# Seven-product pairs moved to other places in the second feed-forward matrix and in the first step for v

## The chip, the cores and the metric

One core of one Trainium2 chip runs the whole program. The metric is the device time of one execution in microseconds (us). The kernel before takes 2172.05 us, the median of 3 runs (2170.63 to 2173.68).

## The reference

For 256 tokens of width 2048 in float32, a transformer block with two mixers is followed by a gated mixer block. Of the many matrix products only three stretches matter here:

- feed-forward input: `silu(h Wg) * (h Wu)`, with h (256 x 2048) and two matrices of 2048 x 5632;
- feed-forward output: `x = x + ff W2`, with ff (256 x 5632) and W2 (5632 x 2048);
- second block: `h = rmsnorm(x)`, then `h [u | v | gate]`, a matrix of 2048 x 12288 of which the v part (2048 x 4096) is computed first, and an output product.

Between the last two lies an RMS norm over the rows of x: h is x transposed, times a gain by channel, and the factor by token is applied to the products' results.

## The kernel before, in words

**Weights.** Every matrix streams through a ring of four slots (`raw`, RING = 4). A *unit* is 256 rows by 512 columns (512 KB). For unit n, SyncE's queue issues the load of `raw` (L460) once `lo_ready` says that the unit four before it in the same slot has been split (L456). ScalarE (ACT) makes the rounded part `w_hi` (L580), VectorE (DVE) the remainder `w_lo` (L1109), and TensorE (PE) multiplies: each float32 product is three matmuls (hi x hi, hi x lo, lo x hi; `three`, L2059). ACT and DVE work four units ahead: at place j of a step they split unit j + 4. ACT does it only when PE has used unit j (`unit_used`), since that frees the slot's `w_hi`.

**Pairs.** In the feed-forward and in the second block, units come in pairs u (units 2u and 2u + 1: the same 256 rows, two blocks of 512 columns). A *plain pair* (`plain_pair`, L2072) is 8 products of 128 x 128 by 128 x 512, 24 matmuls. A *mixed pair* (`mixed_pair`, L2110) gets the same result from seven products of sums of blocks, 21 matmuls. For that DVE makes four sums of weight blocks (`weight_sums`, L1511: `t_sum`, L1528 to L1531; one of them is written back into `raw`), ACT rounds them (`t_hi`, L919), and DVE takes the remainder (`t_lo`, L1541). On the activation side there are sums too. Where the operand is h they are made once, when a block of rows is turned: `stat_hi` (L854, L858) on ACT, `stat_lo` (L1447, L1451 to L1454) on DVE, `mixed_hi` (L864) on ACT, `mixed_lo` (`s_lo`, L1461) on DVE, whose `op_ready` tells PE that the block is there. Where the operand is ff they are made for each mixed pair: `sf_sum` (L1523 to L1526), `sf_hi` (L922), `sf_lo` (L1544); PE waits for `sf_ready` ahead of the pair's second unit (L2130). `weight_sums` for pair u runs at place j = 2u - 4, and needs both units of the pair in `raw`; `t_lo` and `sf_lo` follow at place 2u - 3. Plain pairs of the feed-forward output also need `ff_hi` (L579) and `ff_lo` (L1108), one of each for two units.

**Which pairs are mixed** is written out by hand. The feed-forward output (segment FFN_OUT) has 2 steps of 22 pairs (44 units), with the mixed pairs in `MIXED_OUT`. The product for v (V_IN) has 4 steps of 8 pairs (16 units): `MIXED` = (2, 4, 6), but (4, 6) in step 0. Three PSUM regions gather the mixed products; after a step's last mixed pair, ACT and DVE copy and add them (`parts`, L926 and L1546), and DVE adds them to x (`rows_with_parts`, L1574). At the end of the step `rows_whole` (L1586) adds the rest from the accumulators `gp` and gives them free for the next step.

**Turning x.** The four blocks of 512 columns of x are ready two by two: blocks 0 and 1 when step 0 of FFN_OUT ends, blocks 2 and 3 when step 1 ends. So blocks 0 and 1 are turned in step 1 of FFN_OUT, and 2 and 3 in step 0 of V_IN. PE transposes a block at a place written by hand (`turn_x`, L2012, at the end of unit j = 1 and of unit j = 4, `turn_rows`, L2159; 8 transposes, L1994). It waits for `op_ready` of the blocks before, since the block's sums share buffers, and ACT and DVE take it up at hand-written places behind their own splits: `rows_hi` (L965) and `rows_lo` (L1637). The first mixed pair of a step waits in `shared_banks` (L2089) for all the turned blocks, because the transposes go through the same PSUM banks as the mixed products. In V_IN every pair u also waits for its own rows of h (L2143).

**The token factor** for v needs the squares of all four blocks of x: `squares(3)` on ACT, `mean_square` and `token_scale` on DVE, a square root on ACT between them, all at hand-written places in `v_first` (L993, L1658). Its user is the evacuation of V_IN's first step.

Of the kernel before, what the change touches and what calls it, by code (L numbers as in the profile page):

```python
# [48 lines left out]
MIXED = (2, 4, 6)  # L49
MIXED_FIRST = (4, 6)  # L50
MIXED_LAST = (2, 4)
MIXED_OUT = ((3, 7, 11, 15, 19), (6, 10, 14, 18))
PLACES = 3


# [38 lines left out]
def build(nc, x, w_in, b_gate, norm_mix, norm_ffn, lb_logits, out_gain, q_gain, k_gain, rel_bias,  # L94
# [3 lines left out]
    with ctx:  # L98
# [254 lines left out]
        QF, IV, G_IN, QK, GATES, PROJ_A, PROJ_B, OUT, FFN_IN, FFN_OUT, V_IN, UG_IN, Y_OUT = range(len(S))  # L353
# [7 lines left out]
        op0, hi0, n, n_hi = {}, {}, 0, 0  # L361
# [5 lines left out]
        TURN_M, TURN_H2, TURN_FF, TURN_H3, TURN_Y = 0, 4, 8, 8 + S[FFN_IN].steps, 12 + S[FFN_IN].steps  # L367
# [14 lines left out]
        def mixed(k, i):  # L382

            if k == FFN_OUT:
                return MIXED_OUT[i]
            if isinstance(i, int) and i == 0 and k != UG_IN:
                return MIXED_FIRST
            if isinstance(i, int) and i == S[k].steps - 1 and k == UG_IN:
                return MIXED_LAST
            return MIXED  # L390

        done_steps, done_pairs = {}, {}
        for k in (FFN_IN, FFN_OUT, V_IN, UG_IN):
            done_steps[k] = sum(S[q].steps for q in done_steps)
            done_pairs[k] = sum(len(mixed(q, i)) for q in done_pairs for i in range(S[q].steps))
# [5 lines left out]
        def pairs(k, i, n):  # L401

            if isinstance(i, int) and i == 0:
                return n + done_pairs[k]
            return i * len(MIXED) + (n + len(mixed(k, 0)) - len(MIXED) + done_pairs[k])

        def last_unit(k, i):

            return 2 * mixed(k, i)[-1] + 1
# [17 lines left out]
        def sums_made(i, n):  # L427

            return (0, len(MIXED_OUT[0]))[i] + n + 1

# [135 lines left out]
        def _(act):  # L566
# [71 lines left out]
            def rms(dst, src, dim):  # L638

                return act.activation(dst, src, ACT.Sqrt, scale=1.0 / dim, bias=eps_c[0:dst.shape[0]])  # L640
# [192 lines left out]
            def scaled_rows(k, i, b):  # L833

                act.wait_ge(bank_free[b], freed(k, i + 1))
                n = 2 * i + b
                for t in range(TB):
                    ins = act.activation(xs_tok[:, t], x_tok[:, t, n * NB:(n + 1) * NB], ACT.Copy, scale=rx[:, t:t + 1])
                ins.then_inc(xs_ready, 1)

            def squares(n):

                for t in range(TB):
                    ins = act.activation(wide4[:, t * NB:(t + 1) * NB], x_tok[:, t, n * NB:(n + 1) * NB], ACT.Square,
                                         accum_out=ssf[:, t, n:n + 1])
                own.link(ins)
                if n == 3:
                    act.sem_inc(sq_ready, 1)

            def stat_hi(n, turn, gain):  # L850

                act.wait_ge(tile_turned, turn + n + 1)
                for m in range(4):
                    ins = act.activation(a_hi[:, 4 * n + m], turn_b[:, m], ACT.Copy, scale=col(gain + 4 * n + m))  # L854
                if n:
                    act.wait_ge(op_ready, op0[FFN_IN if turn == TURN_H2 else V_IN] + 4 * n)
                    for m in range(UK):
                        ins = act.activation(a_two[:, m], turn_b[:, m], ACT.Copy, scale=col(gain + 4 * n + m))  # L858
                ins.then_inc(tile_hi, 1)

            def mixed_hi(n, turn):

                act.wait_ge(s_summed, n + (3 if turn == TURN_H3 else 0))
                act.activation(s_hi[:, n - 1], s_sum[:], ACT.Copy).then_inc(s_hi_ready, 1)  # L864
# [100 lines left out]
            def rows_hi(n, j):  # L965

                if j == 0:
                    scaled_rows(FFN_OUT, n // 2, 0)
                if j == 1:
                    stat_hi(n, TURN_H3, GAIN_A)  # L970
                    scaled_rows(FFN_OUT, n // 2, 1)
                if j == 2:
                    squares(n)
                if j == 3 and n:
                    mixed_hi(n, TURN_H3)
                if j == 5:
                    stat_hi(n + 1, TURN_H3, GAIN_A)
                    squares(n + 1)
                if j == 6:
                    mixed_hi(n + 1, TURN_H3)  # L980

            def fo_first(i, j):
                if j == 3:
# [2 lines left out]
            def fo_second(i, j):  # L986
                rows_hi(0, j)
# [4 lines left out]

            def v_first(i, j):  # L993
                rows_hi(2, j)
                if j == 8:
                    act.wait_ge(sums2, 2)
                    rms(r_tok, tot, D).then_inc(rstd_ready, 1)
                if j == 10:
                    act.wait_ge(scale_ready, 2)
                if j == 2:  # L1000
                    act.wait_ge(ws_turned, 1)
                    act.activation(ws_t[:, 1].rearrange("p g n -> p (g n)"), mx[:, 0:2].rearrange("p a n -> p (a n)"),
                                   ACT.Copy).then_inc(ws_copied, 1)
# [95 lines left out]
        def _(dve):  # L1099
# [342 lines left out]
            def stat_lo(n, turn, gain):  # L1442

                dve.wait_ge(tile_hi, turn + n + 1)
                for m in range(4):
                    one = 4 * n + m
                    ins = dve.scalar_tensor_tensor(out=a_lo[:, one], in0=turn_b[:, m], scalar=col(gain + one),  # L1447
                                                   in1=a_hi[:, one].bitcast(F32), op0=ALU.mult, op1=ALU.subtract)
                if n:
                    a11, a21, a12, a22 = a_two[:, 0, 0:P], a_two[:, 0, P:T], a_two[:, 1, 0:P], a_two[:, 1, P:T]  # L1450
                    own.link(dve.tensor_tensor(s_sum[:, 0], a21, a22, ALU.add))  # L1451
                    dve.tensor_tensor(s_sum[:, 2], a11, a21, ALU.subtract)
                    own.link(dve.tensor_tensor(s_sum[:, 1], s_sum[:, 0], a11, ALU.subtract))
                    dve.tensor_tensor(s_sum[:, 3], a12, s_sum[:, 1], ALU.subtract).then_inc(s_summed, 1)  # L1454
                else:
                    ins.then_inc(op_ready, 4)

            def mixed_lo(n, turn):

                dve.wait_ge(s_hi_ready, n + (3 if turn == TURN_H3 else 0))  # L1460
                dve.tensor_tensor(s_lo[:, n - 1], s_sum[:], s_hi[:, n - 1].bitcast(F32), ALU.subtract).then_inc(op_ready, 4)  # L1461
# [21 lines left out]
            def mean_square(r):  # L1483

                dve.wait_ge(sq_ready, 2 + r)
                own.link(dve.tensor_reduce(tot, ssf, AX_X, ALU.add))
                dve.sem_inc(sums2, 1)

            def token_scale(r):

                dve.wait_ge(rstd_ready, 2 + r)
                if r == 0:
                    dve.reciprocal(rf, rx)
                own.link(dve.reciprocal(r_tok, r_tok))
                dve.tensor_tensor(r_tok, r_tok, rf, ALU.mult).then_inc(scale_ready, 1)
# [141 lines left out]
            def rows_lo(n, j):  # L1637

                if j == 2:
                    stat_lo(n, TURN_H3, GAIN_A)  # L1640
                if j == 3 and n:
                    mixed_lo(n, TURN_H3)
                if j == 5:
                    stat_lo(n + 1, TURN_H3, GAIN_A)
                if j == 6:
                    mixed_lo(n + 1, TURN_H3)

            def fo_first(i, j):
# [3 lines left out]
            def fo_second(i, j):  # L1652
                rows_lo(0, j)
# [3 lines left out]

            def v_first(i, j):  # L1658
                rows_lo(2, j)
                if j == 7:  # L1660
                    mean_square(1)
                if j == 9:
                    token_scale(1)

            double_step(V_IN, 0, nothing, v_first)
# [105 lines left out]
        def _(pe):  # L1771
# [218 lines left out]
            def turn(src):  # L1990

                for m in range(4):
                    for t in range(TB):
                        ins = pe.transpose(turn_b[:, m, t * P:(t + 1) * P], src(t, m), ident[:])  # L1994
                ins.then_inc(tile_turned, 1)
# [16 lines left out]
            def turn_x(k, i, b, done):  # L2012

                n = 2 * i + b
                pe.wait_ge(op_ready, done + 4 * n)
                if k == OUT:
                    pe.wait_ge(xs_ready, n + 1)
                else:
                    pe.wait_ge(xs_ready, n + 5)
                    pe.wait_ge(tile_hi, TURN_H3)  # L2020
                turn(lambda t, m: xs_tok[:, t, m * P:(m + 1) * P])
# [136 lines left out]

            def turn_rows(i, j):  # L2159

                if j in (1, 4):
                    turn_x(FFN_OUT, i, j // 4, op0[V_IN])

            def fo_first(i, j):
                if j == 3:
# [2 lines left out]
            def fo_second(i, j):  # L2168
                turn_rows(0, j)
# [65 lines left out]
```

## Time and profile before

| | |
|---|---|
| median of 3 runs | 2172.05 us (2170.63 to 2173.68) |
| profiled execution, its own time | 2171.42 us |
| its span | 2169.7 us |
| PE busy | 2149.2 us (99%), 10394 matmuls |
| DVE busy | 1718.5 us (79%) |
| ACT busy | 1257.2 us (58%) |
| DMA | 412.36 MB, mean 190 GB/s |
| mean granted TensorE clock | 0.997 |

PE is busy nearly all the time by this count, so the time is the number of its matmuls times their distance, plus the places where it waits. In the span FFN_OUT lies from about 1213 to 1452 us, and the first step of V_IN from about 1452 to 1508 us. In the rows below, a start is in us from the span's start, and `[0.69 <-DVE x_tok L1586]` is the idle time of the engine ahead of that row and what ended it.

### The profile page before, as it was taken

What the parts mean: (1) busy time and instruction counts of PE and PEld (TensorE: products, weight loads), DVE (VectorE), ACT (ScalarE), POOL (GpSimd) and SP (SyncE); (2) the same over time, 40 slices, a digit from 0 to 9 for tenths busy, and PEclk for the clock granted to TensorE, in tenths of its full rate; (3) what the DMA queues carried; (4) which work ended last, traced back from release to release, by engine and by line L of the source; (5) the groups of instructions that cost most, each with busy time, mean ns of one, the idle gap of its engine ahead of it and who ended that gap; (6) DMA issues with size and microseconds to landing.
All of it is one profiled execution on the core that took longest, in us unless ns stands there. A gap on an engine that the chain in (4) does not pass through costs nothing.

```text
span 2169.7 us, 30892 instructions
## 1 busy us (share of the span) xinstructions
PE 2149.2 (99%) x10394; PEld 1805.2 (83%) x10394; DVE 1718.5 (79%) x2087; ACT 1257.2 (58%) x1475; POOL 134.3 (6%) x218
## 2 busy tenths in 40 slices
PE   9999999999999999999999999999999999999997
PEld 9988988788888888888888888887888888888886
DVE  5466788666665699999899888878889999998775
ACT  5364355456544665555555566566667666666664
POOL 2021433201000000000000000000000000000000
PEclk9999999999999999999999999999999999999999
DMA  7666555566556666666666666565666666656664
GB/s 247 186 202 192 156 146 148 176 219 182 179 184 189 180 205 201 199 196 195 203 185 206 198 193 195 183 209 159 204 209 190 186 194 196 191 180 211 192 194 141
DMA packets 211499, 412.36 MB, mean 190 GB/s; under 512 B 13161, under 2 KB 13265, under 8 KB 211281
## 3 DMA queue, kind: packets, MB, share of 16 engines
q1 hardware_dynamic: 208592, 402.70, 60.2%
q0 software_dynamic: 1920, 5.31, 0.7%
q10 hardware_dynamic: 896, 3.15, 0.4%
q8 instruction: 55, 0.90, 0.2%
q14 instruction: 36, 0.29, 0.0%
HBM read 409.01 MB, written 3.16 MB: 190 GB/s over the span
## 4 chain that ended last, share of the span: by engine, by line
PE 92%; DVE 5%; DMA 1%; ACT 1%; issue 0%; DVEq 0%; SPq 0%; ACTq 0%
PE gp L2062 39%; PE gp L1793 39%; PE mx L2062 9%; DVE w_lo L1109 2%; PE mx L1994 1%; DMA raw<-w_ffn_out_in 1%; PE mx L1885 1%; PE mx L2043 1%; DVE ff_lo L1108 1%; DVE t_lo L1541 0%; ACT w_hi L580 0%; PE mx L1896 0%; ACT a_hi L854 0%; PE mx L1888 0%; DMA x_tok<-x_in 0%
## 5 line engine op out<-in xcount | busy, mean ns | idle before, releaser
L580 ACT ACTIVATE w_hi<-raw 128x1024 fp32r<-128x1024 f32 x760 | 798.4, 1056 | 709.4 <-PE gp L1793 302.2
L1109 DVE TENSOR_TENSOR w_lo<-raw,w_hi 128x1024 fp32r<-128x1024 f32 x760 | 924.4, 1231 | 268.3 <-ACT w_hi L580 260.0
L2062 PE MATMUL gp<-w_hi,a_hi 128*128 128x512 f32 x1010 | 396.7, 393 | 0.0
L2062 PE MATMUL gp<-w_lo,a_hi 128*128 128x512 f32 x1010 | 393.5, 390 | 0.0
L2062 PE MATMUL gp<-w_hi,a_lo 128*128 128x512 f32 x1010 | 393.4, 390 | 0.0
L1793 PE MATMUL gp<-w_hi,a_hi 128*128 128x512 f32 x576 | 230.2, 400 | 0.0
L1793 PE MATMUL gp<-w_lo,a_hi 128*128 128x512 f32 x576 | 224.7, 390 | 0.0
L1793 PE MATMUL gp<-w_hi,a_lo 128*128 128x512 f32 x576 | 224.3, 389 | 0.0
L2062 PEld LDWEIGHTS gp<-w_hi,a_hi 128*128 128x128 f32 x1010 | 189.8, 188 | 41.0 <-issue 2.7
L2062 PEld LDWEIGHTS gp<-w_lo,a_hi 128*128 128x128 f32 x1010 | 189.7, 188 | 40.0
L2062 PEld LDWEIGHTS gp<-w_hi,a_lo 128*128 128x128 f32 x1010 | 189.8, 188 | 38.2
L1541 DVE TENSOR_TENSOR t_lo<-t_sum,t_hi 128x1536 fp32r<-128x1536 f32 x75 | 131.7, 1756 | 9.0 <-ACT t_hi L919 5.3
L1793 PEld LDWEIGHTS gp<-w_lo,a_hi 128*128 128x128 f32 x576 | 108.1, 188 | 23.2
L1793 PEld LDWEIGHTS gp<-w_hi,a_hi 128*128 128x128 f32 x576 | 108.2, 188 | 22.0 <-issue 0.4
L1793 PEld LDWEIGHTS gp<-w_hi,a_lo 128*128 128x128 f32 x576 | 108.3, 188 | 21.2
L2062 PE MATMUL gp<-w_hi,ff_hi 128*128 128x512 f32 x289 | 113.0, 391 | 1.0 <-DVE x_tok L1586 0.7
L2062 PE MATMUL gp<-w_lo,ff_hi 128*128 128x512 f32 x289 | 112.5, 389 | 0.0
L2062 PE MATMUL gp<-w_hi,ff_lo 128*128 128x512 f32 x289 | 112.5, 389 | 0.0
L919 ACT ACTIVATE t_hi<-t_sum 128x1536 fp32r<-128x1536 f32 x75 | 110.5, 1473 | 0.8 <-PE gp L2062 0.8
L1793 PE MATMUL gp<-a_hi,w_hi 128*128 128x256 f32 x384 | 109.7, 286 | 0.6 <-DVE w_lo L1109 0.6
L1793 PE MATMUL gp<-a_hi,w_lo 128*128 128x256 f32 x384 | 108.7, 283 | 0.0
L1793 PE MATMUL gp<-a_lo,w_hi 128*128 128x256 f32 x384 | 108.6, 283 | 0.0
(369 smaller groups left out, 3481.7 us busy)
## 6 DMA issues: line engine op xcount, KB each, us to landing
raw<-a_w_in_in SPq DMA_DIRECT2D x192, 512.0 KB, 4.5
raw<-w_in_in SPq DMA_DIRECT2D x176, 512.0 KB, 3.8
raw<-w_ffn_in_in SPq DMA_DIRECT2D x176, 512.0 KB, 4.5
raw<-w_ffn_out_in SPq DMA_DIRECT2D x88, 512.0 KB, 4.7
raw<-a_w_out_in SPq DMA_DIRECT2D x64, 512.0 KB, 4.7
raw<-w_out_in SPq DMA_DIRECT2D x32, 512.0 KB, 4.0
raw<-w_proj_a_in SPq DMA_DIRECT2D x16, 512.0 KB, 4.4
raw<-w_proj_b_in SPq DMA_DIRECT2D x16, 512.0 KB, 4.6
```

What stands on the lines that cost most here:

```text
L580: act.activation(w_hi[:, slot], raw[:, slot], ACT.Copy).then_inc(hi_ready, 1)
L919: act.activation(t_hi[:], t_sum[:], ACT.Copy).then_inc(t_hi_ready, 1)
L1108: dve.tensor_tensor(lo[:, place], src, hi[:, place].bitcast(F32), ALU.subtract)
L1109: dve.tensor_tensor(w_lo[:, slot], raw[:, slot], w_hi[:, slot], ALU.subtract).then_inc(lo_ready, 1)
L1541: dve.tensor_tensor(t_lo[:], t_sum[:], t_hi[:].bitcast(F32), ALU.subtract).then_inc(t_lo_ready, 1)
L1793: ins = pe.matmul(out_, stat, mov, start=start, stop=last and p == 2, skip_group_check=True)
L1885: pe.matmul(part8[:, (l + 1) * P:(l + 2) * P], decay[buf][:, l, tb], decay[buf][:, l, tb], start=True, stop=True, skip_group_check=True)
L1994: ins = pe.transpose(turn_b[:, m, t * P:(t + 1) * P], src(t, m), ident[:])
L2043: ins = pe.matmul(mx[:, c // 2, t0:t0 + P], v_one[:, b, c * P:(c + 1) * P], ws_t[:, b, bass.ds(g, 1)].rearrange("p a n -> p (a n)"), start ...
L2062: ins = pe.matmul(out_, stat[sp_], mov[mp], start=start and p == 0, stop=stop and p == 2, skip_group_check=True)
```

## The change

In FFN_OUT step 0 the mixed pairs go from 3, 7, 11, 15, 19 to 3, 6, 10, 14, 17 (five as before), and in step 1 from 6, 10, 14, 18 to 9, 12, 15, 18 (four as before). In V_IN step 0 they go from 4, 6 to 6 alone. The second block of rows turned in each of the two stretches is turned after unit 6 in place of unit 4. ACT's and DVE's parts of it move along, and so do the places of the token factor.

```diff
-MIXED_OUT = ((3, 7, 11, 15, 19), (6, 10, 14, 18))
+MIXED_OUT = ((3, 6, 10, 14, 17), (9, 12, 15, 18))
+MIXED_V = (6,)
...
             if isinstance(i, int) and i == 0 and k != UG_IN:
-                return MIXED_FIRST
+                return MIXED_V if k == V_IN else MIXED_FIRST
...
             def rows_hi(n, j):
...
-                if j == 5:
+                if j == 7:
                     stat_hi(n + 1, TURN_H3, GAIN_A)
+                if j == 8:
+                    mixed_hi(n + 1, TURN_H3)
                     squares(n + 1)
-                if j == 6:
-                    mixed_hi(n + 1, TURN_H3)
...
             def v_first(i, j):
                 rows_hi(2, j)
-                if j == 8:
+                if j == 11:
                     act.wait_ge(sums2, 2)
                     rms(r_tok, tot, D).then_inc(rstd_ready, 1)
-                if j == 10:
+                if j == 13:
                     act.wait_ge(scale_ready, 2)
...
             def rows_lo(n, j):
...
-                if j == 5:
+                if j == 8:
                     stat_lo(n + 1, TURN_H3, GAIN_A)
-                if j == 6:
+                if j == 9:
                     mixed_lo(n + 1, TURN_H3)
...
             def v_first(i, j):
                 rows_lo(2, j)
-                if j == 7:
+                if j == 10:
                     mean_square(1)
-                if j == 9:
+                if j == 12:
                     token_scale(1)
...
             def turn_rows(i, j):
-                if j in (1, 4):
-                    turn_x(FFN_OUT, i, j // 4, op0[V_IN])
+                if j in (1, 6):
+                    turn_x(FFN_OUT, i, j // 6, op0[V_IN])
```

## Rows read from the trace of the kernel before

**Rows 1.** Timeline of PE around its four waits of over 0.5 us: start, us, instruction

```profile
1333.60 0.39 PE L2062 MATMUL gp<-w_lo,ff_hi 128*128 128x512 f32 x1
1334.67 0.50 PE L2062 MATMUL gp<-w_hi,ff_hi 128*128 128x512 f32 x1 [0.69 <-DVE x_tok L1586]
...
1367.71 0.39 PE L2062 MATMUL gp<-w_lo,ff_hi 128*128 128x512 f32 x1
1369.19 0.47 PE L2062 MATMUL mx<-w_hi,sf_hi 128*128 128x512 f32 x1 [1.09 <-DVE sf_lo L1544]
...
1467.45 0.39 PE L2062 MATMUL gp<-w_lo,a_hi 128*128 128x512 f32 x1
1469.06 1.09 PE L1994 MATMUL mx<-ident,wide 128*128 128x128 f32 x8 [1.22 <-DVE s_lo L1461]
...
1477.97 0.39 PE L2062 MATMUL gp<-w_lo,a_hi 128*128 128x512 f32 x1
1482.23 0.77 PE L2062 MATMUL mx<-w_hi,a_hi 128*128 128x512 f32 x1 [3.88 <-DVE s_lo L1461]
```

**Rows 2.** Chain of waits, step 1 of FFN_OUT: start, us, what

```profile
1372.19 17.00 PE gp L2062 x75
...
1391.91 1.36 PE mx L2062 x6
```

**Rows 3.** Windows of PE: us, busy time by engine, granted clock, DMA share, GB/s

```profile
1482.20:1487.30 5.10, 5.07 (x12) 4.03 (x13) 4.79 (x7) 2.05 (x2) 0.00 (x0) 0.51 0.66 206
...
1367.00:1372.00 5.00, 3.91 (x17) 2.93 (x16) 5.00 (x6) 4.39 (x6) 0.00 (x0) 1.00 0.62 204
```

**Rows 4.** Timeline of DVE, step 0 of FFN_OUT: `sf_lo` of pair 3, sums of 7 and 19

```profile
1231.01 0.68 DVE L1544 TENSOR_TENSOR sf_lo<-sf_sum,sf_hi 128x512 fp32r<-128x512 f32 x1
...
1243.78 0.28 DVE L1523 TENSOR_TENSOR sf_sum<-ff 128x128 f32<-128x128 f32 x1
...
1252.64 0.69 DVE L1108 TENSOR_TENSOR ff_lo<-ff,ff_hi 128x512 fp32r<-128x512 f32 x1
...
1307.38 0.29 DVE L1523 TENSOR_TENSOR sf_sum<-ff 128x128 f32<-128x128 f32 x1 [0.21 <-DMA raw<-w_ffn_out_in]
```

**Rows 5.** SyncE's queue: load issued after the second split behind pair 7's `sf_lo`

```profile
1255.76 0.37 SPq L460 DMA_DIRECT2D raw<-w_ffn_out_in  x1
```

**Rows 6.** DMA issues, one load each (issued 1235.08, 1392.65, 1434.77, 1475.52 us): last number is us to landing

```profile
raw<-w_ffn_out_in SPq DMA_DIRECT2D x1, 512.0 KB, 4.8
...
raw<-w_ffn_out_in SPq DMA_DIRECT2D x1, 512.0 KB, 4.3
...
raw<-w_ffn_out_in SPq DMA_DIRECT2D x1, 512.0 KB, 5.7
...
raw<-a_w_in_in SPq DMA_DIRECT2D x1, 512.0 KB, 3.9
```

**Rows 7.** Timeline of PE: start of the second unit of mixed pair 3, step 0

```profile
1232.45 0.39 PE L2062 MATMUL mx<-w_hi,sf_hi 128*128 128x512 f32 x1
```

**Rows 8.** Timeline of DVE, end of FFN_OUT step 0

```profile
1323.74 2.50 DVE L1574 TENSOR_TENSOR x_tok<-c_part,x_tok 128x512 f32<-128x512 f32 x4
...
1333.34 1.28 DVE L1586 TENSOR_TENSOR x_tok<-gp,x_tok 128x512 f32<-128x512 f32 x2
```

**Rows 9.** Timeline of ACT and of DVE, step 0 of V_IN

```profile
1473.04 1.06 ACT L580 ACTIVATE w_hi<-raw 128x1024 fp32r<-128x1024 f32 x1 [4.05 <-PE gp L2062]
1474.00 1.47 ACT L919 ACTIVATE t_hi<-t_sum 128x1536 fp32r<-128x1536 f32 x1
...
1468.92 0.68 DVE L1528 TENSOR_TENSOR t_sum<-raw 128x512 f32<-128x512 f32 x1
...
1475.51 1.76 DVE L1541 TENSOR_TENSOR t_lo<-t_sum,t_hi 128x1536 fp32r<-128x1536 f32 x1 [0.15 <-ACT t_hi L919]
1477.68 1.66 DVE L1447 SCALAR_TENSOR_TENSOR a_lo<-mx,vec,a_hi 128x256 fp32r<-128x256 f32 x4 [0.42 <-ACT a_two L858]
...
1480.31 1.22 DVE L1109 TENSOR_TENSOR w_lo<-raw,w_hi 128x1024 fp32r<-128x1024 f32 x1
```

## The prediction

> **What bounds the kernel now.** I read the page first: PE is busy 99% of the span, so the time is the number of matmuls times their distance, plus what PE waits. Then I read the chain of waits in a stretch of FFN_OUT where nothing disturbs it: 75 matmuls take 17.00 us, and 6 more 1.36 us [rows 2]. That is 0.2267 us for a matmul of 512 columns: 2.72 us for a plain unit (12), 5.44 for a plain pair (24), 4.76 for a mixed pair (21). A mixed pair is worth 0.68 us. Last, I read PE's timeline from the end of the feed-forward input to V_IN for starts that are further apart than that. Apart from a wait of 0.3 us at FFN_OUT's start, which the change does not reach, there are four [rows 1]:
>
> - 1333.60 to 1334.67, for the second accumulator of step 1: 1.07 less 0.23 is 0.84 us;
> - 1367.71 to 1369.19, for `sf_lo` of the first mixed pair (6) of step 1: 1.25 us;
> - 1467.45 to 1469.06, transposes of block 3 waiting for `s_lo` of block 2: 1.38 us;
> - 1477.97 to 1482.23, the first mixed pair (4) of V_IN waiting for `s_lo` of block 3: 4.03 us. Behind it the granted clock is 0.51, the lower level (1.2 GHz), until 1487.3: 12 matmuls take 5.10 us [rows 3]. At full clock they would take 2.72, so the fall costs 2.4 us more. Behind the 1.25 us wait the clock stayed at 1.00 [rows 3].
>
> The first matmul after a wait also lasts 0.47 to 0.50 us in place of 0.39 [rows 1], so each of the two short ones costs 0.1 more. Together some 10 us can be had here, and the change addresses all four.
>
> **What it takes away, and what hides the moved work.** Five and four mixed pairs stay in FFN_OUT: no matmul more or less. V_IN loses one: three matmuls more, 0.68 us. Both block turns stay, eight transposes each. In FFN_OUT step 1 the second turn moves two units down, and its share on ACT and DVE too. The first mixed pair is now 9, its sums come at place 14, and ACT's and DVE's parts of the turn end at places 8 and 9. PE's plain pairs cover these, so they cost nothing, and the 1.35 us wait goes. ACT delays its splits there by about the turn's work, less than 7 us, while it works four units (10.9 us) ahead.
>
> In step 0 the last mixed pair moves from 19 to 17. DVE's work behind it, four additions into `c_part` and then four into x (2.50 us) [rows 8], now lies two pairs (10.9 us) earlier. In the old place it pushes DVE's splits against the end of the step, so that the last addition into x starts at 1333.34 and PE waits for it [rows 1, 8]. The last unit of the step ends about 2.7 us before the 1333.8 at which PE wants that accumulator. The addition takes 1.28 us, and DVE is caught up. So 0.84 + 0.1 = 0.95 us goes. Sum so far: 0.95 + 1.35 = 2.3 us gained.
>
> **What it adds: mixed pairs three apart.** Before, they are four apart. Now 3 to 6, 14 to 17, 9 to 12, 12 to 15 and 15 to 18 are three apart. Follow DVE from one pair's `sf_lo` to the next's. `weight_sums` needs the second unit of its pair in `raw`. With distance three, that load may start only when the *second* split behind the last `sf_lo` is done; with distance four it is the fourth split. The pieces:
>
> - from the instruction behind `sf_lo` (1252.64) to the issue of that load (1255.76): 3.12 us [rows 4, 5];
> - issue to landing. Seven loads in this place took 4.3 to 5.7 us, mean 5.2 [rows 6]; they share the engines with the loads issued around them. About 0.1 more to DVE's start;
> - sums, two splits, `t_lo` and `sf_lo`: 1243.78 to 1252.64 is 8.86 us [rows 4].
>
> That is 17.3 us a cycle (16.4 to 17.8). DVE's other two splits fit in the shadow of the load. PE needs 4.76 + 2 x 5.44 = 15.64 us. So PE waits 1.65 us, and with 0.1 for the restart 1.75, at each mixed pair that follows at distance three and starts with no slack. At distance four DVE takes (1307.38 - 1243.78) / 3 = 21.2 us [rows 4] where PE needs 21.08: even, 0.1 each.
>
> Step 0: `sf_lo` of pair 3 ends at 1231.69 and PE takes the unit at 1232.45 [rows 4, 7]. PE starts 0.15 us behind an `sf_lo` that it waits for, so the slack is 0.6. For pair 6 the load is the one issued at 1235.08 that took 4.8 us [rows 6]: sums at 1240.0, `sf_lo` done at 1248.9, PE at 1249.1. It wanted 1232.45 + 15.64 = 1248.1. That is 1.0 + 0.1. Pairs 10 and 14: 0.2. Pair 17: 1.75. Together 3.05 us. Step 1: pair 9 comes with the same slack of 0.6, pair 12 costs 1.75 - 0.6 = 1.15, pairs 15 and 18 cost 1.75 each: 4.65 us. Sum of the additions 7.7 us. With the short loads (cycle 16.4) it is about 3.3, with the long ones (17.8) about 11.
>
> **V_IN, step 0.** Unit 4 ends at 1467.7. Before, PE is at full work again at about 1487.3, has done mixed pair 4, pair 5 follows, and mixed pair 6 starts. I add it up: 1467.7 + 1.38 (wait) + 0.9 (turn) + 3 x 2.72 + 4.1 (wait) + 4.76 + 2.4 (clock) + 5.44 + 4.76 = 1499.6 for the end of pair 6. Now the transposes no longer wait, since `s_lo` of block 2 is done at 1469 [rows 1]. Units 5 and 6 end at 1473.1, the turn at 1474.0, unit 7 at 1476.75, and mixed pair 6 is wanted at 1487.65. It needs `s_lo` of block 3, and that goes round like this:
>
> - ACT, place 7: split of unit 11, only after unit 7 is used, 1476.9 to 1477.95 (1.06 [rows 9]); then `stat_hi`, 2.2 us, to 1480.1;
> - DVE, place 8: its `weight_sums` for pair 6 come first, after the split of unit 11 ends at 1479.15. Four operations of 0.68 [rows 9] reach to 1481.85, the split of unit 12 to 1483.0, then `stat_lo`, 1477.68 to 1480.31 [rows 9], 2.63 us, to 1485.65;
> - ACT, place 8: `mixed_hi` waits for that, to 1486.25, `squares` 1.4 us, to 1487.6; place 9: split of unit 13 to 1488.65, `t_hi` (1.4) to 1490.05. It was queued behind the wait;
> - DVE, place 9: split to 1489.85, `t_lo` (1.7) from 1490.1 to 1491.8, and only then `s_lo`, 0.6 us, to 1492.4.
>
> PE starts pair 6 at 1492.5, a wait of 4.85 us, longer than the one that was there, and I expect the clock to fall again (2.4). End of pair 6: 1492.5 + 4.76 + 2.4 = 1499.7. V_IN gains nothing (0 +- 0.5): the one long wait takes up what both had, and the lost pair's 0.68. The token factor comes three places later, at 1495.6, before its first user; nothing waits.
>
> **Sum:** -2.3 + 7.7 + 0 = +5.4 us on the profiled execution's own 2171.42, which stands 0.6 under the median of 2172.05. On the median that makes 2177.4 us. Ends of the unknown costs: +1 and +8.7, with V_IN's half on either side.
>
> **A rule against this.** The two ends hang on the loads' time to landing. The row to hold against the seven is a load of V_IN that goes alone, 3.9 us [rows 6]. The Trainium skill (DMA: Bandwidth & Descriptors, Anatomy of one DMA) gives a fixed 2.0 us plus the bytes over 436 GB/s, for loads issued by GpSimd; for 512 KB an estimate of 3.2 us. By that the cycle would be 15.3 us, under PE's 15.64, and the sum would be -2.3. No load here is that short; the rival below takes the shortest kind that the trace has.
>
> **Rivals.** (A) *The loads land like lone ones.* Closer mixed pairs change which transfers overlap; at 3.7 to 3.9 us the cycle is 15.8 to 16.0, the first of each step is free and the others cost 0.2 to 0.35: together under 1. Then -2.3 + 0.7 = -1.6, 2170.4 us. Not slower. It decides if landing is under some 4 us. Against it: seven of seven loads in this place took over 4.2. (B) *The clock does not fall in V_IN.* 5.4 - 2.4 = +3.0, 2175.0. Against it: a wait of 3.9 us idle made it fall, and the new one is longer. With A as well it is -4.0, about 2168. (C) *The waits of 1.75 us make it fall too.* For it: between 1.25 (no fall) and 4.03 (fall) the trace shows nothing. Against it: they are nearer the lower. Two such falls add 4.8 us: 2182.
>
> **How the numbers follow.** A measurement of this kernel tells about 0.2% (4.3 us) from no change. My forecast has 0.60; its own range is 2173 to 2181, of which 0.42 lies over 0.2% slower (2176.4) and 0.18 within. A has 0.14 (0.11 same, 0.03 faster), B 0.09 (0.05 same, 0.04 slower), A with B 0.06 (0.03 and 0.03), C 0.07 (slower), all else 0.04, faster. Faster 0.10, same 0.37, slower 0.53. The range takes A and stops short of C and of A with B: 2170 to 2181.
>
> **What would show it.** PE idle rows in front of the second unit of pairs 6, 17, 12, 15 and 18, released by `sf_lo`, 0.8 to 2 us each, with sums released by DMA; no wait at the start of step 1 nor at its pair 9; one wait on `s_lo` of nearly 5 us in V_IN, and 0.5 as clock behind it; 10397 matmuls. It is wrong if `sf_lo` comes in time at distance three, if `s_lo` comes clearly before 1490, or if other stretches move.

## The result, and the profile after

| | before | after |
|---|---|---|
| median | 2172.75 us (2170.63 to 2173.68, 5 runs) | 2181.84 us (2179.59 to 2186.47, 5 runs) |
| profiled execution: span | 2169.7 us | 2178.0 us |
| matmuls | 10394 | 10397 |

The ratio is 1.0047 (of the means; the medians give 1.0042), with a 95% interval of 1.0032 to 1.0062: slower, by 9.1 us in the medians and by 8.3 us between the two profiled spans. The profiled execution of the changed kernel is the fastest of its five. The forecast was +5.4 us, 2177.4 in a range of 2170 to 2181. The sign was right; the time lies 0.8 us over the range, and 5.4 us is below the interval, which is 7.0 to 13.5 us.

The waits of PE in the changed kernel, longest in total first (releaser, total us, times, longest; its lines are one further than those of before):

```profile
PE mx L2063 <- DVE sf_lo L1545: 5.9, 5, 1.8
PE mx L2063 <- DVE s_lo L1462: 5.0, 1, 5.0
...
PE mx L2063 <- DVE w_lo L1110: 0.9, 1, 0.9
```

Against [rows 1], the wait for x at the start of step 1 is gone, and so is the one at the turn in V_IN. Waits for `sf_lo` went from one of 1.1 us idle to five with 5.9, one for a plain `w_lo` is new, and the two for `s_lo` are one of 5.0. PE's timeline says where (start, us, instruction, idle ahead of it):

```profile
1247.96 0.39 PE L2063 MATMUL gp<-w_lo,ff_hi 128*128 128x512 f32 x1
1248.85 0.47 PE L2063 MATMUL mx<-w_hi,sf_hi 128*128 128x512 f32 x1 [0.50 <-DVE sf_lo L1545]
...
1269.83 0.39 PE L2063 MATMUL gp<-w_lo,ff_hi 128*128 128x512 f32 x1
1270.64 0.47 PE L2063 MATMUL mx<-w_hi,sf_hi 128*128 128x512 f32 x1 [0.43 <-DVE sf_lo L1545]
...
1307.22 0.39 PE L2063 MATMUL gp<-w_lo,ff_hi 128*128 128x512 f32 x1
1309.12 0.47 PE L2063 MATMUL mx<-w_hi,sf_hi 128*128 128x512 f32 x1 [1.51 <-DVE sf_lo L1545]
...
1385.67 0.39 PE L2063 MATMUL gp<-w_lo,ff_hi 128*128 128x512 f32 x1
1387.00 0.47 PE L2063 MATMUL mx<-w_hi,ff_hi 128*128 128x512 f32 x1 [0.94 <-DVE w_lo L1110]
...
1388.22 0.39 PE L2063 MATMUL gp<-w_lo,ff_hi 128*128 128x512 f32 x1
1390.40 0.47 PE L2063 MATMUL mx<-w_hi,sf_hi 128*128 128x512 f32 x1 [1.80 <-DVE sf_lo L1545]
...
1439.16 0.39 PE L2063 MATMUL gp<-w_lo,ff_hi 128*128 128x512 f32 x1
1441.17 0.47 PE L2063 MATMUL mx<-w_hi,sf_hi 128*128 128x512 f32 x1 [1.62 <-DVE sf_lo L1545]
...
1496.15 0.39 PE L2063 MATMUL gp<-w_lo,a_hi 128*128 128x512 f32 x1
1501.49 0.76 PE L2063 MATMUL mx<-w_hi,a_hi 128*128 128x512 f32 x1 [4.95 <-DVE s_lo L1462]
```

Each gap from start to start, less the 0.23 us of a matmul, is what the wait costs: 0.66 at pair 6 of step 0, 0.58 at 10, 1.67 at 17; in step 1, 1.10 and 1.95 at pair 9, nothing at pair 12, 0.2 at pair 15 and 1.78 at 18; 5.11 in V_IN. A new gap of 0.44 us stands in front of the turn behind unit 1 of step 1 (1340.27). The prediction had nothing at pair 9, 1.15 at 12 and 1.75 at 15. The clock fell behind two of the waits (window, us, busy time by engine, granted clock, DMA share, GB/s):

```profile
1390.40:1395.00 4.60, 4.59 (x14) 3.63 (x15) 4.60 (x6) 2.76 (x4) 0.00 (x0) 0.65 0.62 185
...
1501.40:1506.40 5.00, 4.91 (x16) 4.00 (x17) 3.25 (x4) 2.69 (x5) 0.00 (x0) 0.70 0.60 176
```

From its first product to its last, FFN_OUT takes 8.7 us longer than before; of this, 1.6 is the low clock behind pair 9. The low clock in V_IN cost 1.4 us. V_IN gives 0.7 back by the first mixed pair of its step 1. Behind it the two traces differ by 0.3 us more.

Why does pair 9 come late, where the forecast saw no wait at all? The rows of ACT and of DVE in step 1, first ACT, then DVE:

```profile
1362.31 1.09 ACT L581 ACTIVATE w_hi<-raw 128x1024 fp32r<-128x1024 f32 x1
1367.90 0.63 ACT L865 ACTIVATE s_hi<-s_sum 128x512 fp32r<-128x512 f32 x1 [4.51 <-DVE s_sum L1455]
...
1369.80 1.06 ACT L581 ACTIVATE w_hi<-raw 128x1024 fp32r<-128x1024 f32 x1
```

```profile
1370.89 1.23 DVE L1110 TENSOR_TENSOR w_lo<-raw,w_hi 128x1024 fp32r<-128x1024 f32 x1 [3.02 <-ACT w_hi L581]
1372.03 0.69 DVE L1462 TENSOR_TENSOR s_lo<-s_sum,s_hi 128x512 fp32r<-128x512 f32 x1
1372.63 0.68 DVE L1109 TENSOR_TENSOR ff_lo<-ff,ff_hi 128x512 fp32r<-128x512 f32 x1
1373.23 2.35 DVE L1110 TENSOR_TENSOR w_lo<-raw,w_hi 128x1024 fp32r<-128x1024 f32 x2
1375.51 0.68 DVE L1109 TENSOR_TENSOR ff_lo<-ff,ff_hi 128x512 fp32r<-128x512 f32 x1
1376.11 2.35 DVE L1110 TENSOR_TENSOR w_lo<-raw,w_hi 128x1024 fp32r<-128x1024 f32 x2
1381.32 0.29 DVE L1524 TENSOR_TENSOR sf_sum<-ff 128x128 f32<-128x128 f32 x1 [2.86 <-DMA raw<-w_ffn_out_in]
```

At place 8 ACT sits in `mixed_hi` for 4.51 us until DVE has made the block's sums. `squares` and the split of unit 13 stand behind it. DVE in turn waits 3.02 us for that split's `w_hi`, then does five splits almost without a gap. Each split sets off a load, so the loads of units 17 to 21 go out late, all within 6.5 us; that of unit 19 is issued at 1375.75 and lands 5.5 us later. Pair 9 is units 18 and 19, its sums wait for exactly that load, and PE waits for the pair's `w_lo` and its `sf_lo`.

### The profile page after: what moved, and what is told of

It reads as the page before. It is cut to its first block, busy times and chain, and to the rows that moved or that the text cites. A ratio compares the mean times of both kernels' runs of the same rounds, so it can differ in the third digit from the quotient of the medians.

```text
span 2178.0 us, 30890 instructions
## 1 busy us (share of the span) xinstructions
PE 2151.9 (99%) x10397; PEld 1806.2 (83%) x10397; DVE 1714.1 (79%) x2082; ACT 1254.5 (58%) x1474; POOL 134.7 (6%) x218
## 4 chain that ended last, share of the span: by engine, by line
PE 89%; DVE 6%; DMA 3%; issue 1%; ACT 1%; SPq 0%; DVEq 0%; ACTq 0%
PE gp L1794 38%; PE gp L2063 38%; PE mx L2063 8%; DVE w_lo L1110 2%; DMA raw<-w_ffn_out_in 2%; PE mx L1995 1%; PE mx L1886 1%; PE mx L2044 1%; DVE t_lo L1542 1%; DVE ff_lo L1109 1%; DMA raw<-w_ffn_in_in 1%; DVE t_sum L1532 0%; DVE raw L1530 0%; DVE t_sum L1529 0%; PE mx L1897 0%
```

## The experiments

Theory 1 has three parts. (a) A mixed pair that follows at distance three waits for its own second unit's load. (b) Pair 9 of step 1 is late by the block turn's new places. (c) In V_IN the turn's chain and the mixed pair's weight sums stand in each other's way, and moving both keeps the conflict. The rivals are in the expectations. Intervals in brackets are 95%, and a single kernel's difference is known to 2 or 3 us. Where a median is set against the kernel before, it is that of the runs on the same chip.

### Each part alone

Step 0's pairs:

```diff
-MIXED_OUT = ((3, 7, 11, 15, 19), (6, 10, 14, 18))
+MIXED_OUT = ((3, 6, 10, 14, 17), (6, 10, 14, 18))
```

> The kernel before with the pairs of FFN_OUT step 0 alone moved (3, 6, 10, 14, 17). Theory 1 (each pair that follows at distance three waits for its own sums, since the load of its second unit may start only behind the second split): waits of 0.7 at pair 6, 0.7 at 10, 1.7 at 17, less the 0.95 us at the step's end: +2.2 us, 1.001. Rival (distance three costs nothing by itself, and the waits seen in step 0 come from something in the other parts of the change): -0.9 us.

Measured 2174.93 us against 2172.87, ratio 1.0010 (1.0001 to 1.0019), +2.1 us. Waits of 1.2 at pair 6 and 1.8 at pair 17, and the wait for the accumulator at step 1's start gone; 0.4 us in its place, at the turn behind unit 1. The 0.7 us expected at pair 10 did not come. The rival's -0.9 us lies outside the interval. The forecast of the prediction for this part was 3.05 - 0.95 = +2.1.

Step 1's pairs with block 1's turn (places of n = 0 alone):

```diff
-MIXED_OUT = ((3, 7, 11, 15, 19), (6, 10, 14, 18))
+MIXED_OUT = ((3, 7, 11, 15, 19), (9, 12, 15, 18))
...
-                if j in (1, 4):
-                    turn_x(FFN_OUT, i, j // 4, op0[V_IN])
+                if j in (1, (6, 4)[i]):
+                    turn_x(FFN_OUT, i, int(j > 1), op0[V_IN])
```

> The kernel before with step 1's pairs (9, 12, 15, 18) and the turn of block 1 two units later. Theory 1 (the block turn: ACT waits in mixed_hi at place 8 for DVE's sums, the split of unit 13 stands behind it, four loads are issued in a bunch, and pair 9 comes late): two waits at pair 9 of 1.1 and 2.0 with 1.6 us of low clock behind them, 0.2 and 1.8 at 15 and 18, less the 1.35 us of pair 6: +5.5 us, 1.0025. Rival (distance three alone): pair 9 in time, 12, 15 and 18 at 1.75 each: about +3.5 us, with the waits at 12, 15 and 18.

Measured 2178.78 against 2172.87, ratio 1.0030 (1.0019 to 1.0040), +5.9 us. Its waits for `sf_lo`:

```profile
PE mx L2065 <- DVE sf_lo L1547: 7.1, 4, 1.8
...
PE mx L2065 <- DVE w_lo L1112: 0.8, 1, 0.8
```

Both theory and rival had a piece of the truth: 1.0 and 2.0 us at pair 9, *and* 1.8, 2.0 and 2.0 us at 12, 15 and 18. The clock fell behind the last of them, where it did not fall behind the three before it, which were as long. The profiled execution is the second longest of the eight (2181.98 against a median of 2178.78), so its waits add up to more than the 5.9 us.

V_IN's part (pair 6 alone mixed, block 3 turned behind unit 6, its places and the token factor's as in the change):

```diff
+MIXED_V = (6,)
...
-                return MIXED_FIRST
+                return MIXED_V if k == V_IN else MIXED_FIRST
...
-                if j in (1, 4):
-                    turn_x(FFN_OUT, i, j // 4, op0[V_IN])
+                if j in (1, (4, 6)[i]):
+                    turn_x(FFN_OUT, i, int(j > 1), op0[V_IN])
```

> The kernel before with V_IN step 0 alone changed (pair 6 alone mixed, block 3 turned behind unit 6, all places moved). Theory 1 (one wait of 5 us for s_lo with a fall of the clock takes up what both waits cost, since DVE's weight sums and ACT's wait in mixed_hi now stand ahead of s_lo): -0.7 us, 1.000. Rival (the new places are free of waits and what was lost came from FFN_OUT): -7 us, 0.997.

Measured 2174.03 against 2172.87, ratio 1.0005 (0.9996 to 1.0014): not to be told from no change. One wait of 5.1 us and the low clock behind it. The three parts add up to 2.1 + 5.9 + 1.2 = 9.2 us, beside the whole change's 9.1. Each term is known to some 2 us only, so this shows no large interaction and doesn't rule out one of 2 or 3 us.

### What makes pair 9 late

The same pairs, the turn left in its old place:

```diff
-MIXED_OUT = ((3, 7, 11, 15, 19), (6, 10, 14, 18))
+MIXED_OUT = ((3, 7, 11, 15, 19), (9, 12, 15, 18))
```

> The kernel before with step 1's pairs at 9, 12, 15, 18, but block 1 turned where it was, places as before. Theory 1 (pair 9's late sums come from the moved turn, the waits at 12, 15 and 18 from distance three): no wait over 0.3 us at pair 9, 1.2 at 12, 1.8 at 15 and 18, less the 1.35 of pair 6: +3.5 us, 1.0016. Rival (pair 9 is late for another reason): waits at pair 9 as in s1_only, 1.0 and 2.0, and the same time as s1_only, +6 us.

Measured 2175.10 against 2172.75, ratio 1.0011 (1.0001 to 1.0020), +2.4 us. No wait at pair 9. Its waits for `sf_lo` are now three, which cost 1.7, 2.0 and 0.5 us at 12, 15 and 18. The clock fell behind the second, and PE, slowed by 1.6 us, waited only 0.5 us at pair 18:

```profile
PE mx L2062 <- DVE sf_lo L1544: 3.7, 3, 1.8
```

```profile
1420.00:1425.00 5.00, 5.00 (x15) 4.00 (x16) 5.00 (x6) 2.74 (x4) 0.00 (x0) 0.66 0.68 209
```

So the late pair 9 belongs to the turn's place and not to the pair's, and it is worth 5.9 - 2.4 = 3.5 us, with some 3 us on either side, as two measurements go into it. The traces of the two kernels agree: at pair 9 PE waits 3.0 us in `s1_only` and nothing here. They also show what the turn's place delays. The load of unit 19, the last that pair 9 needs, is issued at 1374.77 in `s1_only` and at 1369.73 here. Step 1 starts 1.3 us later in the trace of `s1_only`, so the load goes out 3.7 us later. It takes no longer to land, first `s1_only`, then `s1_pairs`:

```profile
raw<-w_ffn_out_in SPq DMA_DIRECT2D x1, 512.0 KB, 5.4
```

```profile
raw<-w_ffn_out_in SPq DMA_DIRECT2D x1, 512.0 KB, 5.3
```

So pair 9 is late because the load is issued late, and not because the loads stand close together. The next run asks which engine's order does it. It is the whole change with ACT's `mixed_hi` and `squares` one place later, behind the split of unit 13:

```diff
-                if j == 8:
+                if j == 9:
                     mixed_hi(n + 1, TURN_H3)
                     squares(n + 1)
```

> The changed kernel with ACT's mixed_hi and squares one place later, behind the split of unit 13 (place 9). Theory 1 (the order on ACT is what delays pair 9 of step 1 and s_lo of block 3): the waits at pair 9 go (3 us and 1.6 of low clock), s_lo in V_IN comes 3.3 us sooner: -6 to -8 us against the changed kernel, about 2174 to 2176, at 1.001 of the kernel before. Rival (DVE alone is late, ACT's order does not matter): same as the changed kernel, 1.004.

Measured 2176.59 (11 runs) against 2172.87, ratio 1.0013 (1.0004 to 1.0022): +3.7 us, where the whole change has +9.1. The wait for `w_lo` is gone and V_IN's wait is 1.6 in place of 5.1 us, with the clock at full speed behind it:

```profile
1496.00:1503.00 7.00, 5.55 (x25) 4.29 (x24) 5.75 (x8) 6.80 (x10) 0.00 (x0) 1.00 0.56 167
```

At pair 9 one wait of 1.8 us stays, where the expectation had them all gone: DVE still does four splits in a row there (1371.65 to 1377.6), and the sums still wait 2.35 us for the last load. ACT, too, still waits in `mixed_hi`, 2.72 us in place of 4.51, now with the split of unit 14 behind it; how the rest divides between this and the turn's work on DVE was not tried. So the order on ACT makes the larger part of pair 9's lateness: 3.05 us of waits and 1.6 of low clock became 1.8 us. But FFN_OUT as a whole got no shorter, 247.4 us from its first product to its last against 247.5 in the changed kernel's trace: pairs 12, 15 and 18 wait 2.0, 1.4 and 1.4 us here, against 0.0, 0.2 and 1.8 there. In the traces V_IN has 4.8 us of what this kernel gained, 3.5 of wait and 1.4 of low clock; the medians are 5.3 us apart.

### What the distance costs, and by what

The whole change with mixed pairs four apart:

```diff
-MIXED_OUT = ((3, 6, 10, 14, 17), (9, 12, 15, 18))
+MIXED_OUT = ((3, 7, 11, 15, 19), (9, 13, 17))
```

> The changed kernel with mixed pairs four apart: 3, 7, 11, 15, 19 in step 0 and 9, 13, 17 in step 1 (one mixed pair fewer: 0.7 us more of matmuls). Theory 1 (distance three): no wait over 0.6 us at any pair but 9, which keeps its 3 us: +4.6 us against the kernel before, 1.0021, some 4 us under the changed kernel. Rival (the waits at the later pairs are an echo of the late start at pair 9, not of the distance): waits of 1 us and more at 13 and 17 too, +7 us or more.

Measured 2175.20 against 2172.75, ratio 1.0010 (1.0000 to 1.0019), +2.5 us, where +4.6 was expected; the clock did not fall behind pair 9 here. Pair 9 waits its 0.8 and 2.0 us, and no other pair of FFN_OUT waits over 0.25 us:

```profile
PE mx L2066 <- DVE s_lo L1465: 5.0, 1, 5.0
PE mx L2066 <- DVE sf_lo L1548: 1.8, 1, 1.8
...
PE mx L2066 <- DVE w_lo L1113: 0.7, 1, 0.7
```

The waits are not an echo of pair 9: it is the distance. That leaves whether DVE's work or the load is what does not fit. This run takes `s1_pairs` and halves FFN_OUT's loads; the second 128 rows of each unit are not loaded. Every split, sum and matmul is still done, on what the slot held before, so the result is not the product:

```diff
+                    if k == FFN_OUT:
+                        src = s.w[u * UK * P:(u * UK + 1) * P, bass.ds(i * s.stride + c, NB)]
+                        sp.dma_start(raw[:, j % RING, 0], src).then_inc(raw_in[j % RING], 16)
+                        continue
```

> s1_pairs (pairs 9, 12, 15, 18; block 1 turned in the old place), but FFN_OUT's loads bring only the first 128 of a unit's 256 rows, 256 KB in place of 512; the other half of raw keeps what it held, so the feed-forward output is left wrong by that part. All else issues as it did. Theory 1 (the landing of the pair's second unit is the piece of DVE's cycle that does not fit): landing falls by 1 us or more, the cycle to 16 us or less, and the waits at 12, 15 and 18 (1.7, 2.0, 0.5 us there) fall to under 0.4 each. Rival (DVE's own work is too much for 15.64 us): the waits stay over 1 us.

Landings in FFN_OUT (bytes, median us), first this kernel, then `s1_pairs` in the same stretch:

```profile
raw<-w_ffn_out_in SPq DMA_DIRECT2D x40, 256.0 KB, 3.2
```

```profile
raw<-w_ffn_out_in SPq DMA_DIRECT2D x39, 512.0 KB, 5.0
```

No wait for `sf_lo` of 0.25 us or more is left in either step. The second units of pairs 9, 12, 15 and 18 start exactly 15.64 us apart (1385.86, 1401.50, 1417.14 and 1432.78), which is PE's own time for a mixed and two plain pairs. With the same work on DVE, 1.8 us less landing removes it all: theory 1 (a) holds. This doesn't make DVE's work small. In this kernel's cycle from pair 9 to pair 12 it is busy for 14.88 of the 15.64 us (the third busy time):

```profile
1385.86:1401.50 15.64, 15.64 (x70) 12.95 (x69) 14.88 (x20) 9.61 (x11) 0.00 (x0) 1.00 0.30 101
```

It fits, with 0.8 us to spare, and what didn't fit was this work together with the part of a landing that nothing covers. The kernel ran once, with 2172.34 us.

### Whether V_IN has something to give

Pair 6 alone mixed, everything else as in the kernel before, the turn behind unit 4:

```diff
+MIXED_V = (6,)
...
-                return MIXED_FIRST
+                return MIXED_V if k == V_IN else MIXED_FIRST
```

> The kernel before with pair 6 alone mixed in V_IN step 0, block 3 turned where it was (behind unit 4), all places as before. Theory 1 (the turn's own chain of ACT and DVE is 14 us long; what made V_IN slow was the first mixed pair standing in its way): the wait of 4.0 us and the low clock behind it (2.4) go, 1.4 us at the turn stays, three matmuls more (0.7): -5.7 us, 0.9974. Rival (s_lo of block 3 is late whatever stands around it): -1 to +1 us.

Measured 2166.37 against 2172.75, ratio 0.9970 (0.9958 to 0.9982), -6.4 us: faster by 0.3%, with one new line and one changed. In V_IN only the turn's wait is left:

```profile
PE mx L1995 <- DVE s_lo L1462: 1.2, 1, 1.2
PE mx L2063 <- DVE sf_lo L1545: 1.1, 1, 1.1
```

One place later:

```diff
-                if j in (1, 4):
-                    turn_x(FFN_OUT, i, j // 4, op0[V_IN])
+                if j in (1, (4, 5)[i]):
+                    turn_x(FFN_OUT, i, int(j > 1), op0[V_IN])
```

> As v_early, but block 3 is turned behind unit 5, ACT's and DVE's parts one place later. Theory 1: the wait of 1.4 us at the turn goes too: -7.1 us, 0.9967, and no wait on s_lo in V_IN. Rival (one place later the chain runs into the weight sums at place 8, as it does with the turn behind unit 6): a wait on s_lo at pair 6, -3 us or less.

Measured 2166.78 against 2172.75, ratio 0.9971 (0.9960 to 0.9982), -6.0 us. The turn's wait is gone and no wait on `s_lo` came, as theory 1 has it. The median did not fall by the 1.4 us expected, but the two kernels' medians cannot tell 1.4 us. A wait of 0.6 us at the start of V_IN's step 1 is new:

```profile
1501.76 0.49 PE L2066 MATMUL gp<-w_hi,a_hi 128*128 128x512 f32 x1 [0.44 <-DVE c_part L1569]
```

The token factor's places were moved too in this kernel; which of the two made that wait was not tried.

### Better pairs for FFN_OUT

> V_IN as in v_early; step 0's pairs at 2, 6, 10, 14, 18 and step 1's at 7, 11, 15, 19, all four apart, turns and places as before. Theory 1: against v_early the 1.35 us of step 1's first pair and the 0.5 to 0.9 at the end of step 0 go, and the last pair at 19 costs up to 0.9 at the end of step 1: 2165 us, 0.9965. Rival (pair 2 is too early in step 0, behind DVE's last product of the feed-forward input): a wait of 1 us or more at pair 2, no better than v_early.

> As best_a, but step 1's pairs at 9, 13, 17, one fewer (0.7 us more of matmuls). Theory 1: no wait at 9, 13, 17 and none at the end of step 1: 2165 us, 0.9965, within 1 us of best_a. Rival: as for best_a.

```diff
-MIXED_OUT = ((3, 7, 11, 15, 19), (6, 10, 14, 18))
+MIXED_OUT = ((2, 6, 10, 14, 18), (7, 11, 15, 19))
```

(`best_a`; `best_b` has (9, 13, 17) in step 1.) Measured 2169.21, ratio 0.9987 (0.9978 to 0.9996), and 2168.84, 0.9982 (0.9973 to 0.9991): 3 us worse than `v_early`, and 4 us worse than the 2165 expected. The rival had a wait at pair 2 of step 0, and it is there, 2.0 us in `best_a` and 2.1 in `best_b`, not for DVE but for ACT's copy of the last block of ff, whose transposes share the PSUM banks with the mixed products. In `best_a`:

```profile
PE mx L2063 <- ACT ff L909: 1.9, 1, 1.9
```

In `best_b` the clock fell behind it (0.69 in the window 1229.5 to 1235.0). Theory 1 missed more in `best_a`: in step 1, with all pairs four apart, pairs 7, 15 and 19 wait 0.9, 1.3 and 0.4 us for `sf_lo`. The sums of pair 15 waited for a load that was issued at 1402.49 and took 7.7 us. So four apart is no guarantee; what else delays pair 7 was not followed. `best_b` has none of these waits.

With step 0's pairs back at 3, 7, 11, 15, 19:

> V_IN as in v_early, step 0's pairs as in the kernel before (3, 7, 11, 15, 19), step 1's at 9, 13, 17, turns and places as before. Theory 1: against v_early the 1.35 us of step 1's first pair go and three matmuls (0.7 us) come: 2165.7 us, 0.9970, no wait on sf_lo in step 1. Rival (pair 2 was not what cost best_a and best_b 3 us, the pairs of step 1 were): 2168 us or more.

Measured 2166.34 (7 runs) against 2172.51, ratio 0.9969 (0.9958 to 0.9980), -6.2 us, without any wait for `sf_lo` over 0.25 us. That is the 2165.7 expected, and clear of the rival's 2168. It cannot be told from `v_early`. Both beat the kernel before and the changed one, and `v_early` is the smaller edit.

## Why the prediction was right or wrong

**Distance three: the mechanism is right, and so is the size of one wait; the sum for step 1 isn't.** The term was 1.75 us at a pair without slack. Measured: 1.7 and 1.8 (pair 17), 1.8 to 2.0 (12, 15, 18 in `s1_only`), and 1.8 at 18 in the changed kernel. Halving the loads removed it, so the landing is part of it, with DVE's work filling nearly all the rest of the cycle. But in the changed kernel's own trace pairs 12 and 15 waited only 0.2 us or less, where the prediction and its list of signs had 1.15 and 1.75. Behind pair 9 the low clock slowed PE by 1.6 us, and the loads that pairs 12 and 15 needed took 4.7 and 4.4 us. At pair 12 the forecast was 1.15 and `s1_pairs` has 1.7. Pair 9's `sf_lo` ends there at 1384.09 and PE takes the unit at 1384.67, so the slack was 0.4 us where 0.6 had been put in; and the load after it landed in 5.7 us, the long end of the seven, where the mean of 5.2 had been put in. The trace of before has nine loads in this place and not seven, of 4.3 to 5.9 us. The prediction's upper end is also added up wrongly: with a cycle of 17.8 the terms give 10.2 us and not 11, so +7.9 and not +8.7.

**Step 0: right.** +2.1 forecast, +2.1 measured (0.2 to 4.1). The end of the step gave 0.9 us, less 0.4 at the turn, and pair 6 came 0.7 to 1.2 us late where 1.1 was forecast.

**The block turn in FFN_OUT: wrong, and this is the step that failed.** The prediction said: "PE's plain pairs cover these, so they cost nothing". It cost 3.5 us, give or take 3 (`s1_only` less `s1_pairs`); in the traces pair 9 waits 3.0 us with the turn in the new place and nothing with it in the old one, and in the changed kernel 3.05 us, with 1.6 of low clock behind. The sentence on ACT's delay compared it with the 10.9 us that ACT works ahead of PE, and stopped there. But a split on DVE also starts the load of the unit four later, so a delay on ACT is not used up by the lead. It comes back four units later as late loads: that of unit 19 went out 3.7 us later and took as long as before to land (5.4 and 5.3 us). The same wait of ACT in `mixed_hi` was followed step by step for V_IN, where it gave the right answer; in step 1 of FFN_OUT it was not followed.

**V_IN: right in mechanism.** Wait 4.85 forecast, 5.11 measured; the fall of the clock came, but cost 1.4 us where 2.4 had been put in from the trace of before. Net 0 +- 0.5 forecast, -0.7 in the trace and +1.2 (-0.9 to +3.0) in `v_only`. The prediction also worked out what stood in the way, which is the reason that `v_early` could be written down with a number: -5.7 forecast, -6.4 measured.

**The clock in waits of 1.75 us (rival C, given 0.07): true in part.** It fell behind 1.95 us at pair 9 here, 1.6 us of cost, behind one of four such waits in `s1_only` and behind one of two in `s1_pairs`. That the rival's 2182 is the measured time is luck: it counted two such falls of 2.4 us, where the profiled execution has one, of 1.6, and it had nothing for pair 9. The slowest of the five runs, 2186.47, has a mean clock of 0.995, the fastest 0.997; but the next slowest, 2183.92, has 0.997 as well, so what makes the spread stays open. Rival A (short landings) and B (no fall in V_IN) did not happen; the trace of the changed kernel has landings of 3.8 to 6.9 us. 

The Trainium skill's rule for one transfer (DMA: Bandwidth & Descriptors, Anatomy of one DMA), which it gives for GpSimd's path, would have allowed no wait at distance three. The estimates by it, 3.2 us for 512 KB and 2.6 for 256 KB, lie below the 5.0 and 3.2 us measured for SyncE's loads between other loads, so here the trace decides against it.

**The sum:** 5.4 + 3.5 for the turn = 8.9, beside 9.1 measured. That it comes so close is in part luck. In the profiled execution pair 9 cost 4.65 us with its low clock, while pairs 12 and 15 cost 2.7 us less than forecast, the turn behind unit 1 of step 1 cost 0.4 more, and V_IN 0.7 less.

## What to carry to other kernels

In a ring where the split of one unit starts the load of a later one, work that an engine does "in the shadow" is free only if no split is queued behind it. Ask of each inserted wait which load it delays, and who needs that load. Where two chains meet (a block turn and a seven-product pair), moving both by the same amount keeps the collision; taking one away at its price (0.7 us here) gave 6.4 us. And find how close a costly step may follow its like from the cycle of the engine that prepares it: here DVE's work, plus the part of a landing that it doesn't cover, against PE's time.

## What the runs showed of the hardware that was not expected

The granted clock fell behind four waits of 2.0 to 2.1 us of cost: at pair 9 of the changed kernel (with 1.1 us waited just before it), behind the last of four in `s1_only`, at pair 15 of `s1_pairs` and at pair 2 of `best_b`. Each fall cost 1.6 us more. It did not fall behind five waits as long: two in `s1_only`, and one each in `after_hi9`, `after_four` and `best_a`. Waits of this length can go either way. Nor has a fall one price: behind the one long wait in V_IN it cost 2.3 us in the kernel before and 1.4 in the changed one.

One load of 512 KB took 3.65 us alone (changed kernel, issued at 1492.04), up to 6.9 us as the last of four issued within 4 us, and 7.7 us in `best_a`. At the same bytes that is a spread of 3 to 4 us, beside the 1.8 of 5.0 us that halving the bytes of every load saved.
